# Opening stage of a four-layer trunk: input in four transfers, tile and weight splits in turn, squares behind the splits, first half of the values in the score banks

## What is computed

```python
def _rmsnorm(x, g):
    y = x * lax.rsqrt(jnp.mean(x * x, axis=-1, keepdims=True) + RMS_EPS)
    return y * g

# layers 0 and 3, 16 heads of 64
h = _rmsnorm(x, attn_norm[i])
q, k, v = split(h @ w_qkv)
z = q @ k.T * scale                     # per head
valid = key_pos[None, :] < q_pos[:, None]
log_keep = where(valid, log_sigmoid(-z), 0)
att = where(valid, exp(log_sigmoid(z) + cumsum_after(log_keep)), 0)
x = x + (att @ v) @ w_o
x = x + (silu(h2 @ w_gate) * (h2 @ w_up)) @ w_down      # h2 = _rmsnorm(x, ffn_norm[i])
```

## Time and profile before

| | |
|---|---|
| median of 3 runs | 1215.33 us (1215.32 to 1215.5) |
| the profiled execution, its own time | 1215.03 us |
| its span | 1213.1 us |
| PE, DVE, ACT, POOL busy, share of the span | 98%, 62%, 49%, 20% |
| mean granted TensorE clock | 0.998 of full speed |

### The profile page before, as it was taken

One profiled execution on the slowest core, in us unless ns is written; L12 is line 12 of the kernel. 1 busy time (PEld: TensorE's weight loads), 2 busy tenths in 40 slices (PEclk: granted clock), 3 DMA queues, 4 the chain that ended last, 5 costly groups with the idle time before them and its releaser, 6 DMA issues.

```text
span 1213.1 us, 20954 instructions
## 1 busy us (share of the span) xinstructions
PE 1194.2 (98%) x8818; PEld 1116.7 (92%) x8818; DVE 755.5 (62%) x829; ACT 588.8 (49%) x715; POOL 243.2 (20%) x246
## 2 busy tenths in 40 slices
PE   8999999999999999999999999999999999999996
PEld 6999999998997899999899899999889989999985
DVE  7676765555597565656546566556556867656553
ACT  6675444443346544444346544444436755444431
POOL 5000621111123253111111163101110006211121
PEclk9999999999999999999999999999999999999999
DMA  8732455554552245545542245555545334454540
GB/s 319 212 111 105 174 187 196 189 193 174 188 157 105 75 169 209 180 176 201 178 170 105 78 182 203 180 193 179 187 158 201 110 105 174 174 209 174 180 168 35
DMA packets 30839, 202.02 MB, mean 167 GB/s; under 512 B 3504, under 2 KB 4592, under 8 KB 7328
## 3 DMA queue, kind: packets, MB, share of 16 engines
q1 hardware_dynamic: 28800, 197.41, 44.7%
q0 software_dynamic: 352, 1.31, 0.9%
q10 hardware_dynamic: 1600, 2.02, 0.6%
HBM read 197.91 MB, written 1.84 MB: 165 GB/s over the span
## 4 chain that ended last, share of the span: by engine, by line
PE 92%; DVE 3%; ACT 2%; POOL 2%; issue 1%; DMA 0%; ACTq 0%; DVEq 0%; POOLq 0%
PE scores L1161 14%; PE bank L1153 13%; PE bank L1155 13%; PE bank L1154 13%; PE scores L1162 7%; PE scores L1153 7%; PE scores L1154 7%; PE scores L1155 7%; PE scores L1147 3%; PE bank L1147 1%; PE scores L1287 1%; DVE w_lo L742 1%; PE bank L1229 1%; PE scores L1229 1%; POOL sq L314 1%; PE scores L1301 1%
## 5 line engine op out<-in xcount | busy, mean ns | idle before, releaser
L742 DVE TENSOR_TENSOR w_lo<-raw,w_hi 128x2048 fp32r<-128x2048 f32 x183 | 427.0, 2334 | 259.1 <-ACT w_hi L436 258.6
L436 ACT ACTIVATE w_hi<-raw 128x2048 fp32r<-128x2048 f32 x183 | 349.2, 1910 | 176.6 <-PE bank L1155 78.5
L1153 PE MATMUL bank<-x_split,w_hi 128*128 128x256 f32 x1120 | 318.7, 285 | 0.0
L1154 PE MATMUL bank<-x_split,w_hi 128*128 128x256 f32 x1120 | 316.9, 283 | 0.0
L1155 PE MATMUL bank<-x_split,w_lo 128*128 128x256 f32 x1120 | 316.8, 283 | 0.0
L1161 PE MATMUL scores<-hid_split,w_hi 128*128 128x512 f32 x704 | 248.9, 399 | 0.0
L1153 PEld LDWEIGHTS bank<-x_split,w_hi 128*128 128x128 f32 x1120 | 214.7, 192 | 3.5 <-issue 2.4
L1154 PEld LDWEIGHTS bank<-x_split,w_hi 128*128 128x128 f32 x1120 | 214.8, 192 | 0.1
L1155 PEld LDWEIGHTS bank<-x_split,w_lo 128*128 128x128 f32 x1120 | 214.8, 192 | 0.0
L1162 PE MATMUL scores<-hid_split,w_lo 128*128 128x256 f32 x704 | 197.7, 281 | 0.0
L1153 PE MATMUL scores<-x_split,w_hi 128*128 128x256 f32 x672 | 191.1, 284 | 0.0
(11 more groups left out here) (206 smaller groups left out, 1542.8 us busy)
## 6 DMA issues: line engine op xcount, KB each, us to landing
raw<-w SPq DMA_DIRECT2D x183, 1024.0 KB, 4.8
raw<-w SPq DMA_DIRECT2D x8, 256.0 KB, 6.7
x<-x_in SPq DMA_DIRECT2D x2, 512.0 KB, 5.6
raw<-w SPq DMA_DIRECT2D x2, 512.0 KB, 8.5
out<-x SPq DMA_DIRECT2D x4, 256.0 KB, 2.5
k_all<-k_all ACTq DMA_DIRECT2D x1, 960.0 KB, 7.7
rel_scratch<-rel_lut POOLq DMA_DIRECT2D x1, 768.0 KB, 10.6
rel_bias<-rel_scratch POOLq DMA_DIRECT2D x2, 256.0 KB, 7.7
```

The source lines that it names most:

```text
L436: act.activation(w_hi[slot][:, :], raw[slot][:, :], ACT.Copy).then_inc(hi_done, 1)
L742: dve.tensor_tensor(w_lo[slot][:, :], raw[slot][:, :], w_hi[slot][:, :].bitcast(FP32), ALU.subtract).then_inc(lo_done, 1)
L1153: pe.matmul(dst, wh, xh, start=first, stop=False, skip_group_check=True)
L1154: pe.matmul(dst, wh, xl, start=False, stop=False, skip_group_check=True)
```

## The change

SP loads x in four transfers of 256 KB, two tiles each, and each is followed by two pieces of weights. ACT and DVE take one tile and one piece in turn. POOL's squares of layer 0 wait until DVE has finished units 0 and 1. In layer 0, `model_sums(0)` moves from between the halves of the values to a place after the sixth of half 1's eight steps; ACT and DVE split unit 4 before they turn to the sums. In both stick-breaking layers DVE splits unit b + 3 before `mean_square`. Half 0 of the values goes to banks 0 and 1, which `logits(0)` writes later, in place of 4 and 5; the wait for `v_new` moves from before `qk(0)` to before `logits(0)`.

```diff
-SB_V_BANKS = ((4, 5), (2, 3))
+SB_V_BANKS = ((0, 1), (2, 3))
@@ SyncE
-            sp.dma_start(x[:, 0:4, :], x_in[:, 0:4, :]).then_inc(x_loaded[0], 16)
-            for i in range(4):
-                piece(i)
-            sp.dma_start(x[:, 4:8, :], x_in[:, 4:8, :]).then_inc(x_loaded[1], 16)
-            for i in range(4, 8):
-                piece(i)
+            for j in range(PAIRS):
+                sp.dma_start(x[:, 2 * j:2 * j + 2, :], x_in[:, 2 * j:2 * j + 2, :]).then_inc(x_loaded[j], 16)
+                piece(2 * j)
+                piece(2 * j + 1)
@@ GpSimd, model_squares
                     if n == 0:
-                        pool.wait_ge(x_loaded[k // 4], 16)
+                        pool.wait_ge(lo_done, 2)
@@ ScalarE, stick_breaking
                 split(b + 3)
+                if i == 0:
+                    split(b + 4)
                 first_guess(norm, n + 1, 0, SEQ + TOKEN_SUMS[n])
-                split(b + 4)
+                if i:
+                    split(b + 4)
                 value_half(m, b + 2, n, 0)
@@ ScalarE, opening (VectorE the same with norm_lo)
-            for j in range(PAIRS):
-                if j % 2 == 0:
-                    act.wait_ge(x_loaded[j // 2], 16)
-                norm_hi(0, 2 * j)
-                norm_hi(0, 2 * j + 1)
-                split_piece(2 * j)
-                split_piece(2 * j + 1)
+            for k in range(KT):
+                if k % 2 == 0:
+                    act.wait_ge(x_loaded[k // 2], 16)
+                norm_hi(0, k)
+                split_piece(k)
@@ VectorE, stick_breaking
+                split(b + 3)
+                if i == 0:
+                    split(b + 4)
                 mean_square(n)
-                split(b + 3)
                 refine(norm, n + 1, 0, SEQ + TOKEN_SUMS[n], rstd)
-                for u in range(b + 4, b + 7):
+                for u in range(b + 5 if i == 0 else b + 4, b + 7):
                     split(u)
@@ TensorE, stick_breaking
+                            if i == 0 and half == 1 and kk == 5:
+                                model_sums(n)
                         last.then_inc(unit_used, 1)
-                        if half == 0 and kq == 1:
+                        if i and half == 0 and kq == 1:
                             model_sums(n)
...
-                pe.wait_ge(m.v_new, 2)
                 qk(0)
...
                 for p in range(KT):
-                    if p == 1:
-                        pe.wait_ge(m.v_new, 4)
+                    if p < 2:
+                        pe.wait_ge(m.v_new, 2 * p + 2)
                     logits(p)
```

More of the change, by code:

```diff
@@ L216, in trunk @@
         piece_lo = sem("piece_lo")
-        x_loaded = [sem(f"x_loaded{i}") for i in range(2)]
+        x_loaded = [sem(f"x_loaded{i}") for i in range(PAIRS)]
         one_loaded = sem("one_loaded")
@@ L1115, in _ @@
             dve.wait_ge(vec_loaded, 16)
[L1116 to L1122, removed]
+            for k in range(KT):
+                if k % 2 == 0:
+                    dve.wait_ge(x_loaded[k // 2], 16)
+                norm_lo(0, k)
+                split_piece(k)
             split_piece(8)
```

## The result

The changed kernel takes 1219.93 us (median of 6 runs, 1218.94 to 1220.57) against 1215.32 (6 runs, 1215.07 to 1215.5): a ratio of 1.0037 with a 95% interval of 1.0025 to 1.0048, 4.6 us slower. Forecast were 1218.0 and a range of 1214.0 to 1219.6. The direction and the place were right, the size was not. The profiled execution took 1220.08 us, its span is 1217.9, 4.8 more than before.

The account below looks back on a forecast made before the run. PE, busy 98% of the span, was taken as the bound; late squares would make `soft(0)` 2.6 us late. 1215.03 + 2.6 = 1217.7, and as that execution lay 0.3 under the median, 1218.0; range 1214.0 to 1219.6.

Parts of the forecast that it names:

- PE's first matmul near 7.1, half 0 without idle time: Opening: PE starts at about 7.1 and half 0 of the values runs through to 18.1, against 22.5 before.
- Units 0 and 1 done at 14.2: Opening: hi and lo of weight units 0 and 1 finished (`lo_done` 2) at about 14.2, when POOL's squares start.
- ACT and DVE add 1.35: Opening: splitting work of 1.35 us after piece 7 lands at about 12.8, giving units 0 and 1 done at 14.2.
- POOL's chain of 17.1 us with four blocks, 2.0 and 0.9 each: Layer 0's squares: 15 operations, four held up by DVE's lo parts, take 17.1 us from 14.2 and end at 31.3.
- 4.1 us of idle time ahead of the sums: PE, after six steps of half 1, waits from 27.2 to 31.3 for POOL's squares: 4.1 us of new idle time.
- `ms` 1.1 behind the squares: Layer 0: 0.80 us from squares' end to `ms`, plus about 0.3 for three more single-column sums; `ms` at 32.4.
- 15.2 us from `ms` to `soft(0)`, no slack behind: Refinement and ACT's queue put `soft(0)` at 47.6 against 44.99, 2.6 us late; that shift stays to the end.
- PE waiting for q's hi: At `logits(0)`: PE arrives at 44.1 and waits 1.5 us for q's hi, ahead of `soft(0)`.
- Banks, orders, layer 3: nothing: Half 0's banks, the `v_new` wait, POOL's later casts and layer 3's split order cost nothing, bounds -0.1 and +0.1.
- Rival 1: Squares hardly held up: they end by 27.2, PE passes without waiting, time 1213.8, a gain; chance 0.14.
- Rival 3: Clock falls in PE's new 4.1 us wait: sums at half speed take 0.7 us more, 1218.7; chance 0.2.
- Rival 4: Worse: the squares start at 15 or take 19 us, time 1219.5 to 1220.5; chance 0.05.

Follow-up runs that it names:

- experiment 8: The changed kernel, but x loaded in two transfers of 512 KB, four pieces behind each: 1219.27 us, ratio 1.0031 to the kernel before.
- experiment 5: The changed kernel, but DVE makes lo of unit 4 after `mean_square` and not before it: 1218.57 us, ratio 1.0026 to the kernel before.
- experiment 4: The changed kernel, but the sums come after the eighth step of half 1 instead of the sixth: 1218.73 us, ratio 1.0029 to the kernel before.
- experiment 1: The changed kernel, but POOL squares only two of the eight tiles of x in layer 0: 1214.16 us, ratio 0.9993 to the kernel before.
- experiment 3: The changed kernel, but POOL squares each tile of x as it lands, sums in their new place: 1217.49 us, ratio 1.0017 to the kernel before.
- experiment 7: The kernel before with only the new banks, the moved `v_new` wait and DVE's split ahead of `mean_square`: 1215.32 us, ratio 1.0.

## Why the prediction was right in direction and too small in size

The steps, in the order of the prediction:

- **PE's first matmul near 7.1, half 0 without idle time.** 6.58, since the gains landed at 4.68 instead of 5.17; half 0 ran with one short gap. Right.
- **Units 0 and 1 done at 14.2.** Wrong by 1.1: 15.29. This is the first step that failed: "ACT and DVE add 1.35" to a piece 7 landing at 12.8. I let the landing of the last piece set the end of the opening, and took piece 8 as landing when it did before (ACT took it at 15.54, not 14.81). In fact piece 4 held ACT up until 10.94, and from there ACT ran its own chain of four hi parts of pieces and three of tiles without a wait, to 14.47. In experiment 8, where the data moves faster, ACT gets piece 4 at 11.05, and units 0 and 1 are done no sooner.
- **POOL's chain of 17.1 us with four blocks, 2.0 and 0.9 each.** 16.95 us. The blocks are 1.9 to 2.1 and 0.8 to 1.0, and experiment 5 takes one out and gets 2.05. Right. The trace shows why a lo of 2.29 costs POOL less than its length: it is already under way when POOL asks. The addition at 21.60 stands beside a lo from 21.25 to 23.67, and ends 0.60 behind it. The Trainium skill, page "SBUF — State Buffer", section "Who interferes with whom", gives the shared port to whoever issues first, for the whole instruction. The trace agrees; the 1.2 us more that I had drawn from this rule (a chain of 18.3) came of charging the whole lo and not what was left of it.
- **4.1 us of idle time ahead of the sums.** 4.4. Near, but by luck: both its ends came about 1 us later than I had them, PE at 28.1 and not 27.2, the squares at 32.3 and not 31.3.
- **`ms` 1.1 behind the squares.** 2.0. The second step that failed: I kept the fall of the clock as a rival with a chance of 0.2 and a price of 0.7, and the two profiled executions of the changed kernel both show it (2.02 and 1.77), experiment 8 too (2.02), while a wait of 1.6 or 2.4 in experiments 4 and 5 leaves 1.2. How much it costs differs from run to run with the moment at which the clock falls, 31.8 and 32.6 in the two profiles. The Trainium skill, page "TensorE: Matmul & The Clock Gate", section "What's actually happening", lets the phase of the clock differ from run to run; the two profiles agree.
- **15.2 us from `ms` to `soft(0)`, no slack behind.** 15.45 in the changed kernel's first profile, where PE, slowed until 38.6, came late to the logits and ACT waited 0.17 for them; 15.17 in its other profile and in experiments 1, 3, 4 and 8. Right but for 0.3. The sign "PE waiting for q's hi" did not come: of the slack of 1.5 us that I gave PE there, experiments 1 and 3 show 0.8, and matmuls at half speed took all of it in the changed kernel.
- **Banks, orders, layer 3: nothing.** Experiment 7: nothing. Right.

So in the profiled execution 2.6 us became 4.8: 1.0 from the squares' end (a start 1.2 late, a chain 0.15 short), 0.9 from the sums at half speed, 0.3 from PE at half speed behind them. Rival 1 (a gain) would have needed squares that end before 28.7, and they ended at 32.3. Rivals 3 and 4 came true together, and I had given them 0.2 and 0.05. Rival 3, the clock, should have had most of the chance: the new wait that I had worked out was longer than the idle time after which the rows already showed the clock fall. Alone it gave 1218.7. Rival 4 had the squares start at 15, and they started at 15.37; its 1219.5 to 1220.5 holds the measured time, but a start 1.2 late adds 1.2 by my own chain, 1219.2, so the number is right only with the clock's part in it. I had priced each rival as if the others did not happen. The change's own aim, 3.7 us at the start of half 1, was reached. It was lost because the squares are a chain of 17 us in their new place (13.5 in the old one, from 5.04 to 18.58), which ends after PE wants the sum, and because `ms`, which had at least 2.0 us of slack in its old place (experiment 7), has none in the new one.

## What to carry to other kernels

Before deferring a chain of dependent small operations out of the way of a critical stage, add up its length at the new place, with the neighbours that it meets there, and compare its end with the moment at which its result is first needed; then walk the in-order queues behind that result to the next point where the bound engine waits. When two engines hold each other up, as DVE and POOL do here, moving the work in time can merely change who waits; here a third engine with idle slots took it for 0.40 us a tile. And in this kernel a new wait of the TensorE of 4.4 us or more brought half speed in all three profiled executions that had one: the matmuls behind such a wait should be priced at half speed. Last, rivals that can happen together should be added up together.

## What was not expected of the hardware

The clock also fell after shorter idle times than the 4 us that I had read from the end of the program. In experiment 4 it was at half speed from 43.0 to 46.4 after a wait of 2.09 us that ended at 41.72. In the profiled execution of experiment 7 it was there from 9.5 to 12.9, after PE had been idle for 2.2 us before 8.76:

```profile
6.00:9.50 3.50, 1.32 (x6) 0.84 (x5) 3.49 (x4) 3.30 (x7) 3.19 (x5) 1.00 1.01 370
9.50:12.90 3.40, 3.40 (x9) 2.64 (x9) 3.40 (x5) 2.93 (x7) 3.16 (x4) 0.50 1.05 401
12.90:16.00 3.10, 3.10 (x14) 2.27 (x13) 3.10 (x4) 2.11 (x4) 2.79 (x5) 1.00 0.84 300
```

A wait of 2.38 us in experiment 5 did not do it in the profiled execution, whose mean clock is 0.998; two of its nine executions have 0.995, so the clock was at half speed for longer in them. The kernel before has 0.998 in its profiled execution too, but 0.996 in 16 of the 28 executions beside experiment 1, with no more time: whatever stretches of half speed those are, they cost that kernel nothing.

And x in four transfers (rows of 2 KB) instead of two (rows of 4 KB) moved the opening's data more slowly: between 6 and 10 the nine profiles with four transfers have 263 to 301 GB/s, the three with two have 335, 355 and 375. The DMA engines were nearly as busy (0.90 to 0.97 against 0.97 to 1.02). Whether it is the size of the rows or the order of the transfers was not separated.
